# PEER gates through 16-bit one-hots in three parts, a top-16 search over 64 pairs, eleven gathered rows a head, and norms moved in the first and last stage

## What is computed

```python
def block(hc):                                   # 128 tokens at a time
    q = (hc @ wq).reshape(128, 8, 2, 128)
    sc = einsum('thcd,hckd->thck', q, keys)      # 8 heads, 2 halves, 128 keys
    s1, i1 = top_k(sc[:, :, 0], 16)
    s2, i2 = top_k(sc[:, :, 1], 16)
    cand = s1[..., :, None] + s2[..., None, :]   # 256 pairs
    cidx = i1[..., :, None] * 128 + i2[..., None, :]
    top, pos = top_k(cand, 16)
    eidx = take_along_axis(cidx, pos)            # 16 of 16384 experts a head
    gate = softmax(top)
    act = gelu(einsum('thkd,td->thk', u_tab[eidx], hc))
    return einsum('thk,thkd->td', gate * act, v_tab[eidx])
```

## Time and profile before

| | us |
|---|---|
| median of 2 runs | 4164.6 (4156.0 to 4173.3) |
| profiled execution | 4179.5, span 4177.7 |
| PE busy | 3788.4 (91%) |
| DVE busy | 3029.4 (73%) |
| ACT busy, POOL busy | 1375.9, 869.4 |
| granted TensorE clock, mean | 0.949 |

### The profile page before, as it was taken

The page is one execution under the profiler, slowest core; times in us unless marked ns, Lnnn a source line. Parts: engine busy times, 40 slices in busy tenths (PEclk is TensorE's granted clock), DMA queues, the critical chain, the costliest instruction groups (busy, mean ns, idle before and its releaser), DMA issues. The chain is left out here.

```text
span 4177.7 us, 67901 instructions
## 1 busy us (share of the span) xinstructions
PE 3788.4 (91%) x27802; PEld 3460.6 (83%) x27802; DVE 3029.4 (73%) x5310; ACT 1375.9 (33%) x2109; POOL 869.4 (21%) x593
## 2 busy tenths in 40 slices
PE   6878889899998998999999888989999999999997
PEld 4547777699998998999986776669999898899996
DVE  6446455489888987877775646458888897877876
ACT  3442123333333432333334213333333343333332
POOL 3000000011102234444430000001111223544542
PEclk8989989999999999999999989999999999999998
DMA  4741212167776789999961022227777679999994
GB/s 151 262 144 35 99 54 99 61 206 206 208 209 208 270 319 355 338 337 343 349 246 61 22 99 71 91 72 220 211 209 212 213 264 335 359 342 340 338 340 183
DMA packets 319480, 885.61 MB, mean 212 GB/s; under 512 B 29473, under 2 KB 156577, under 8 KB 311745
## 3 DMA queue, kind: packets, MB, share of 16 engines
q1 hardware_dynamic: 245440, 612.80, 43.9%
q0 software_dynamic: 73728, 268.47, 18.0%
HBM read 751.13 MB, written 130.02 MB: 211 GB/s over the span
## 5 line engine op out<-in xcount | busy, mean ns | idle before, releaser
L207 PE MATMUL peer_ps<-peer_h_high,tile_high 128*128 128x384 f32 (+1 forms) x2304 | 797.3, 346 | 35.5 <-DVE peer_h_low L200 16.6
L207 PE MATMUL peer_ps<-gate_high,tile_high 128*128 128x384 f32 x2048 | 709.6, 347 | 96.9 <-DVE tile_low L200 96.8
L2120 POOL DMA_INDIRECT row<-in_peer_u_rows,row_at x256 | 380.9, 1488 | 1969.0 <-DVE row L2352 1202.1
L209 PE MATMUL peer_ps<-peer_h_high,tile_low 128*128 128x384 f32 (+1 forms) x2304 | 788.5, 342 | 0.0
L208 PE MATMUL peer_ps<-peer_h_low,tile_high 128*128 128x384 f32 (+1 forms) x2304 | 788.3, 342 | 0.0
L200 DVE TENSOR_TENSOR tile_low<-tile,tile_high 128x1024 fp32r<-128x1024 f32 x544 | 662.4, 1220 | 157.0 <-ACT tile_high L195 152.2
L208 PE MATMUL peer_ps<-gate_low,tile_high 128*128 128x384 f32 x2048 | 704.0, 344 | 0.0
L209 PE MATMUL peer_ps<-gate_high,tile_low 128*128 128x384 f32 x2048 | 702.9, 343 | 0.0
L195 ACT ACTIVATE tile_high<-tile 128x1024 fp32r<-128x1024 f32 x544 | 571.2, 1050 | 20.1 <-DMA tile<-in_peer_u 19.9
L2120 POOL DMA_INDIRECT row<-in_peer_v,row_at x256 | 454.6, 1776 | 480.0 <-DVE own_sum L2358 437.3
L207 PEld LDWEIGHTS peer_ps<-gate_high,tile_high 128*128 128x128 f32 x2048 | 398.1, 194 | 107.6 <-DVE tile_low L200 107.5
(11 more groups left out here) (453 smaller groups left out, 5476.2 us busy)
## 6 DMA issues: line engine op xcount, KB each, us to landing
tile<-in_peer_u SPq DMA_DIRECT2D x256, 512.0 KB, 4.1
tile<-in_peer_v SPq DMA_DIRECT2D x256, 512.0 KB, 7.1
gates<-gates_out SPq DMA_DIRECT2D x24, 2048.0 KB, 10.1
gates_in<-gates SPq DMA_DIRECT2D x32, 1536.0 KB, 15.9
acts<-up_act SPq DMA_DIRECT2D x240, 192.0 KB, 4.4
act_in<-acts SPq DMA_DIRECT2D x240, 192.0 KB, 8.8
in_w<-in_w_in SPq DMA_DIRECT2D x36, 512.0 KB, 3.6
tile<-in_peer_wq SPq DMA_DIRECT2D x32, 512.0 KB, 4.8
```

The lines of the kernel that those rows point to most:

```text
L207: pe.matmul(out, wh, mh, start=first, stop=False)
L209: return pe.matmul(out, wl, mh, start=False, stop=last)
L2120: pool.indirect_dma_start(row[n % NROW][:, :], None, table, bass.IndirectOffsetOnAxis(ap=row_at[:, n % ROWS:n % ROWS + 1], axis=0)) \
```

## The change

In `peer`: the gate tables are made with 16-bit one-hots. The gate is split into three 16-bit parts that add up to it (`share_gates`, new, four DVE operations a layer), DVE makes one one-hot for each key number and the second times each of the three parts (five operations a group, values laid out keys by tokens, 16 tokens side by side), and PE adds three products a token where there was one. The search for the best 16 of 256 pairs looks at 64 pairs, which hold the best 16 whatever the scores: row 0 with 16, rows 1 to 3 with 8, rows 4 to 7 with 4, rows 8 to 15 with 1. Finding the two key numbers from a position takes other and more small operations. A head takes eleven u rows: six at the sites as before and five in a row at its end (`some_rows(hd, ROWS_BY_HEAD)`), so 77 + 4 + 24 + 16 = 121 come before the down stage and 7 in it; v rows start at tile 10.

In `front`: the products start on activations scaled by the gain alone, and the reciprocal root is multiplied in when DVE, no longer ACT, moves each sum out of PSUM (`take`). The final norm works in two halves of 256 tokens, and its result is stored in eight DMAs.

```diff
+            tile(0)
             for k in range(KD):
                 pe.wait_ge(squared.sem, squared.at(k + 1))
                 last = pe.matmul(ps[7][:, :], pg.c["ones"][:, :], sq[:, k, :], start=(k == 0), stop=(k == KD - 1))
             last.then_inc(summed.sem, 1)
             pe.wait_ge(small_loaded.sem, small_loaded.at(16 * small))
             for j in range(IN_TILES):
-                tile(j)
+                if j:
+                    tile(j)
...
-            def take(j):
-                act.wait_ge(in_summed.sem, in_summed.at(j + 1))
-                i = IN_ORDER[j]
-                if i >= RW_TILES:
-                    act.activation(uT[:, i - RW_TILES, :].rearrange("p (s n) -> p n s", s=SC),
-                                   ps[j % 2][:, :].rearrange("p (n s) -> p n s", s=SC), ACT.Copy).then_inc(in_taken.sem, 1)
-                    return
-                if j >= IN_ZB:
-                    act.wait_ge(shifted.sem, shifted.at(j - IN_ZB + 1))
-                act.activation(zb[j % IN_ZB][:, 1:T + 1], ps[j % 2][:, :], ACT.Copy).then_inc(in_taken.sem, 1)
+            def scaled_high(k):
+                act.activation(rh[:, k, :], pg.xT[:, k, :], ACT.Copy, scale=gain[:, k:k + 1]).then_inc(h_high_made.sem, 1)
...
+            def take(j):
+                i = IN_ORDER[j]
+                dve.wait_ge(in_summed.sem, in_summed.at(j + 1))
+                if i >= RW_TILES:
+                    tokens = lambda x: x.rearrange("p (n s) -> p n s", s=SC)
+                    dve.tensor_tensor(uT[:, i - RW_TILES, :].rearrange("p (s n) -> p n s", s=SC), tokens(ps[j % 2][:, :]), tokens(rstd),
+                                      ALU.mult).then_inc(in_taken.sem, 1)
+                    return
+                if j >= IN_ZB:
+                    dve.wait_ge(shifted.sem, shifted.at(j - IN_ZB + 1))
+                dve.tensor_tensor(zb[j % IN_ZB][:, 1:T + 1], ps[j % 2][:, :], rstd, ALU.mult).then_inc(in_taken.sem, 1)
...
+PLANES = 3
 ROWS = PH * TOPK
 NROW = 6
-ROWS_BY_HEAD, ROWS_BY_GROUP, ROWS_BY_TILE = 6, 1, 1.6
-DOTS_UNTIL = 24
+ROWS_BY_HEAD, ROWS_BY_GROUP, ROWS_BY_TILE = 11, 1, 1.6
+DOTS_UNTIL = 8
+PAIRS = ((0, 1, 16), (1, 3, 8), (4, 4, 4), (8, 8, 1))
+PAIR_AT = [sum(some * wide for _, some, wide in PAIRS[:j]) for j in range(len(PAIRS) + 1)]
+PAIRED = PAIR_AT[-1]
...
-                        last = pe.matmul(ps[2 + n % GBANKS][:, t * NKEY:(t + 1) * NKEY], one[g % 2][:, 4 * c + t, :],
-                                         two[g % 2][:, 4 * c + t, :], start=True, stop=True)
+                        for j in range(PLANES):
+                            last = pe.matmul(ps[2 + n % GBANKS][:, t * NKEY:(t + 1) * NKEY], one[g % 2][:, :, 4 * c + t],
+                                             shares[g % 2][:, j, :, 4 * c + t], start=(j == 0), stop=(j == PLANES - 1))
...
                 dve.tensor_copy(atf[:, :, :, :], at[:, :, :, :])
-                for tb in range(TB):
-                    last = dve.tensor_tensor(cand[:, tb, :, :], down(top[:, tb, 0, :]), across(top[:, tb, 1, :]), ALU.add)
+                at_pair = 0
+                for first, some, broad in PAIRS:
+                    into = cand[:, :, at_pair:at_pair + some * broad].rearrange("p t (a b) -> p t a b", b=broad)
+                    last = dve.tensor_tensor(into, down(top[:, :, 0, first:first + some], broad),
+                                             across(top[:, :, 1, 0:broad], some), ALU.add)
+                    at_pair += some * broad
                 link(last)
                 lows(1)
-                top16([(cand[:, tb, :, :].rearrange("p a b -> p (a b)"), rest[:, tb, :], best[:, tb, own], pos[:, tb, :])
+                top16([(cand[:, tb, :], rest[:, tb, 0:PAIRED], best[:, tb, own], pos[:, tb, :])
                        for tb in range(TB)])
...
-                dve.tensor_scalar(spot[0][:, :, :], pos[:, :, :], 4, None, ALU.logical_shift_right)
-                link(dve.tensor_scalar(spot[1][:, :, :], pos[:, :, :], TOPK - 1, None, ALU.bitwise_and))
-                for j in range(2):
-                    last = dve.tensor_copy(spotf[j][:, :, :], spot[j][:, :, :])
-                link(last)
-                for j in range(2):
-                    for tb in range(TB):
-                        last = dve.tensor_tensor(hit[j][:, tb, :, :], down(spotf[j][:, tb, :]), ramp, ALU.is_equal)
-                link(last)
+                dve.tensor_tensor(steps[:, :, 1:TOPK], atf[:, :, 0, 1:TOPK], atf[:, :, 0, 0:TOPK - 1], ALU.subtract)
+                link(dve.tensor_copy(spotf[0][:, :, :], pos[:, :, :]))
+                dve.tensor_copy(steps[:, :, 0:1], atf[:, :, 0, 0:1])
+                link(dve.tensor_scalar(spotf[1][:, :, :], spotf[0][:, :, :], float(PAIR_AT[1]), None, ALU.is_ge))
+                link(dve.scalar_tensor_tensor(out=spotf[1][:, :, :], in0=spotf[0][:, :, :], scalar=float(PAIR_AT[2]),
+                                              in1=spotf[1][:, :, :], op0=ALU.is_ge, op1=ALU.add))
+                for _ in range(2):
+                    link(dve.scalar_tensor_tensor(out=spotf[1][:, :, :], in0=spotf[0][:, :, :], scalar=float(PAIR_AT[3]),
+                                                  in1=spotf[1][:, :, :], op0=ALU.is_ge, op1=ALU.add))
+                link(dve.tensor_copy(wide[:, :, :], spotf[1][:, :, :]))
+                link(dve.tensor_tensor(spot[:, :, :], mask[:, :, :], wide[:, :, :], ALU.logical_shift_right))
+                link(dve.tensor_tensor(spot[:, :, :], pos[:, :, :], spot[:, :, :], ALU.bitwise_and))
+                dve.tensor_copy(spotf[1][:, :, :], spot[:, :, :])
+                link(dve.tensor_tensor(hit[0][:, :, :, :], down(spotf[0][:, :, :], TOPK), every(starts[:, :]), ALU.is_ge))
                 lows(1)
                 some_rows(hd, 4)
-                for j in range(2):
-                    for tb in range(TB):
-                        last = dve.tensor_tensor(hit[j][:, tb, :, :], hit[j][:, tb, :, :], across(atf[:, tb, j, :]), ALU.mult)
-                link(last)
+                dve.tensor_tensor(hit[1][:, :, :, :], down(spotf[1][:, :, :], TOPK), every(pg.c["ramp"][:, 0:TOPK]), ALU.is_equal)
+                link(dve.tensor_tensor(hit[0][:, :, :, :], hit[0][:, :, :, :], across(steps[:, :, :], TOPK), ALU.mult))
+                link(dve.tensor_tensor(hit[1][:, :, :, :], hit[1][:, :, :, :], across(atf[:, :, 1, :], TOPK), ALU.mult))
                 lows(1)
                 some_rows(hd, 5)
...
+            def share_gates():
+
+                link(dve.tensor_tensor(left[:, :], gate_row[:, :], route[:, 2, :], ALU.subtract))
+                link(dve.tensor_copy(route[:, 3, :], left[:, :]))
+                link(dve.tensor_tensor(left[:, :], left[:, :], route[:, 3, :], ALU.subtract))
+                link(dve.tensor_copy(route[:, 4, :], left[:, :]))
+
             def make_onehots(g):
                 t = slice(g * GROUP, (g + 1) * GROUP)
                 if g >= 2:
                     dve.wait_ge(spread.sem, spread.at((g - 1) * (GROUP // 4)))
-                per_key = lambda j: route[:, j, t].rearrange("p (t k) -> p t k", k=1).to_broadcast([P, GROUP, NKEY])
-                keys_at = pg.c["ramp"][:, :].rearrange("p (t k) -> p t k", t=1).to_broadcast([P, GROUP, NKEY])
-                dve.tensor_tensor(two[g % 2][:, :, :], keys_at, per_key(1), ALU.is_equal)
-                link(dve.tensor_tensor(one[g % 2][:, :, :], keys_at, per_key(0), ALU.is_equal))
-                last = dve.tensor_tensor(two[g % 2][:, :, :], two[g % 2][:, :, :], per_key(2), ALU.mult)
+                per_key = lambda j: route[:, j, t].rearrange("p (k t) -> p k t", k=1).to_broadcast([P, NKEY, GROUP])
+                if g:
+                    dve.wait_ge(onehots_made.sem, onehots_made.at(g))
+                dve.tensor_tensor(two[:, :, :], key_ramp[:, :, :], per_key(1), ALU.is_equal)
+                link(dve.tensor_tensor(one[g % 2][:, :, :], key_ramp[:, :, :], per_key(0), ALU.is_equal))
+                for j in range(PLANES):
+                    last = dve.tensor_tensor(shares[g % 2][:, j, :, :], two[:, :, :], per_key(2 + j), ALU.mult)
                 last.then_inc(onehots_made.sem, 1)
...
             for hd in range(PH):
                 search(hd)
                 lows(BRIDGE + 3 - (PH - 1 - hd) * (UPS_HEAD + 2) - done[0])
+                some_rows(hd, ROWS_BY_HEAD)
...
+            share_gates()
+            link(dve.tensor_copy(key_ramp[:, :, :], pg.c["ramp"][:, :].rearrange("p (k t) -> p k t", t=1)
+                                 .to_broadcast([P, NKEY, GROUP])))
             make_onehots(0)
...
```

More of the change, by code:

```diff
@@ L179, in _, with mean @@
             link = linker(dve, vec_step)
[L180 to L186, removed]
-            link(last)
-    squared.passed(KD)
-    for s in (summed, meaned, rooted):
-        s.passed(1)
+            def mean(h):
+                dve.wait_ge(summed.sem, summed.at(h + 1))
```

(32 more changed lines are left out.)

118 lines of the change are left out of this document (66 added, 52 removed).

## The result

The changed kernel takes **4516.51 us** (median, 4510.91 to 4522.11) against 4164.64 before: the ratio is **1.0845**, 95% interval 1.0732 to 1.0958. The forecast was 4100 with a range up to 4215, so it was wrong in size and in sign. The profiled execution has a span of 4509.2 us, 331.5 more than the 4177.7 before.

The account below looks back on a forecast made before the run. PE was taken as the main bound (91% busy), with DVE close in the one-hot stage and DMA transfers in the down stage. 2 x (-33 - 3 + 8 + 3 - 4) - 7 = -65 us gave 4100 us, range 4050 to 4215.

Parts of the forecast that it names:

- The one-hot stage: One-hot stage of each layer: PE and DVE both near 9.0 us a group after the change, -3 us a layer.
- the price of a gate product: One-hot stage: each one-pass 16-bit product with its own weight load taken at 0.070 us on PE, 48 a group.
- a rival at 0.23 us: One-hot stage: PE's operand reads 32 bytes apart cost about 1.8 ns a value; total +299, 4464 us; chance 0.13.
- Weight loads: One-hot stage: a 16-bit weight load costs PE 0.112 us like a float32 record's; total +27, 4192 us; chance 0.22.
- DVE at one value a cycle: One-hot stage: 16-bit DVE operations get no double pace, 13.8 us a group; total +167, 4332 us; chance 0.04.
- Down stage: Down stage: 35 u row sets a layer move out, easing transfers; 4.35 us for each tile, -33 us a layer.
- Search: Search stage: five rows in a row at a head's end stall PE 1.5 us, seven times; +8 us a layer.
- Bridge: Bridge between search and one-hots: `share_gates` and the wide ramp put DVE work before the first one-hots, +3 us a layer.
- First stage: First stage: PE starts sooner on activations scaled by gain alone, less added waits for `take`; -4 us a layer.
- Last norm: Final norm: two halves hide part of the reciprocal and scaling, and the last DMA is smaller; -7 us once.

Follow-up runs that it names:

- blocks of two tokens: The changed kernel with its 16-bit one-hots held two tokens at a time, one token's values 4 bytes apart for PE instead of 32: 4075.52 us, ratio 0.9804.

## Why the prediction was wrong, by its own steps

**The one-hot stage, forecast -3, measured +208 a layer. The step that failed is the price of a gate product: 0.070 us taken, 0.241 measured.** The sum went from "a pass of 128 columns is 0.056" to the product as if its operands were packed. The distance of the values was put at no cost; it stood in the text only as a rival at 0.23 us (4464 us), with a chance of 0.13, set aside since ACT's and DVE's rows walk 256 bytes a value and TensorE takes a packed float32 value every 0.42 ns. Neither bears on a step of 32 bytes: the cost measured is full from 16 bytes on, and the packed pace says nothing of it. The only strided rows of the trace gave 1.8 ns for both engines, and TensorE's was the same; they should have set the forecast. The rule of the Trainium skill quoted there ("Advanced Engine Details and Errata", SBUF Cachelines) had the right sign: 0.241 us with each value in another line of 16 bytes, 0.056 packed.

The rival itself was 52 us short in all. Its group was 48 x 0.23 + 5.55 = 16.6; with 0.241 it is 17.1 us, 411 a stage. The rest is the clock: behind each group some eight passes start 0.320 and not 0.173 us apart, which with a longer first step is 1.4 us, and 24 times that is 33 us. Together 444, measured 439. No step of mine had a fall of the clock while PE is never idle. What makes the clock fall under these products is not shown.

**Weight loads (0.22)** fell: a load per 16-bit product hides at 0.056 us. What the earlier trace rows shows is a float32 record, 0.112 us for its two passes and loads, half of which is just that 0.056. **DVE at one value a cycle** fell: 1.22 us. The Trainium skill ("VectorE: DVE Perf Modes", the tier table) gives 1224 ns for it, and the trace agrees with 1220.

**The stage before was misread too.** The sum set 9.13 us a group against "the 219 us seen", but 219 is the length of the window in the earlier trace rows, which begins 12 us into the stage. The 32 tiles take 230.6 and 233.3 us, 9.6 to 9.7 a group. With blocks of two tokens, where a product takes 0.058 us (forecast 0.070, bound 0.056), the stage takes 213.8 and 215.3 us, close to the 216 forecast, and DVE's work falls from 9.4 to 8.7 us a group. So at that pace the gain is 17 and 18 us against the kernel before, not 3.

**Down stage, forecast -33, measured -46** (bounds -53 and 0). The mechanism was right, as the run with six rows shows with 46 us by that edit alone. The term was mis-sized: 548.1/128 is 4.28 us a tile and not 4.35. In that the first tile's wait, which I kept at 9.7, is 4.3 in after; with the old one-hots it is 9.1 again and the stage 553.3, so some 5 us of the 46 come with the slow one-hot stage ahead of it.

**Search, forecast +8, measured +21 and +26** (bound +25). "PE stalls 1.5 us, seven times" was too small, and two terms were missing. After's timeline of DVE and PE at a head's end, beside the earlier trace rows:

```profile
1031.68 1.22 DVE L210 TENSOR_TENSOR tile_low<-tile,tile_high 128x1024 fp32r<-128x1024 f32 x1 [4.26 <-ACT tile_high L205]
1032.82 1.22 DVE L2391 SCALAR_TENSOR_TENSOR row<-row,h_own 128x1024 f32<-128x1024 f32 x1
...
1041.66 1.22 DVE L210 TENSOR_TENSOR tile_low<-tile,tile_high 128x1024 fp32r<-128x1024 f32 x1
...
1042.94 0.50 PE L217 MATMUL peer_ps<-peer_h_high,tile_high 128*128 128x512 f32 x1 [2.22 <-DVE tile_low L210]
```

The stall is 2.2 us, and the lead of the tiles behind it, which I called enough, is 1.2 to 2.4 us where six rows leave 4.4 to 5.6, so the whole head runs with less. PE's waits in the search of layer 0, before and then after:

```profile
PE peer_ps L207 <- DVE tile_low L200: 0.5, 1, 0.5
...
PE peer_ps L217 <- DVE tile_low L210: 11.9, 5, 3.5
PE peer_ps L217 <- ACT up_act L2272: 7.2, 9, 1.8
```

So the waits on low parts alone are near the 10 us forecast. What the forecast put at nothing are the longer waits on `up_act` (2.5 before) and the granted clock, 0.98 and 0.97 over the searches of after and 1.00 over those before. By the runs with six and eleven rows the batch cost 19 and not 10; the 64 pairs cost 4 and 8 where I had a gain in DVE's work and none in time.

**Bridge, +3:** +2.9 and +4.3. **First stage, -4:** -5.9 and -5.8; PE's first product now stands 6 us after ACT's first operation, as worked out, and PE waited for `take`'s result (`zb`) once, 0.5 us. Beside the earlier trace rows:

```profile
230.75 2.56 ACT L421 ACTIVATE in_rh<-xT,vec 128x512 fp32r<-128x512 f32 x4 [16.09 <-PEq L1269]
...
236.82 0.80 PE L217 MATMUL front_ps<-in_rh,in_w_high 128*128 128x512 f32 x1 [28.38 <-DVE in_w_low L210]
```

**Last norm, -7:** -6.3; the second half's reciprocal takes 1.67 us in the chain in place of 3.37. The forecast without the one-hots was 2 x (-33 + 8 + 3 - 4) - 7 = -59, and the run with the old ones gave -52 by its ratio. That this agrees is in part luck: the down stage gave more than its term and the search cost more than its own.

## What to carry to other kernels

Price a product by its moving operand's distance in bytes before the number of its columns: in these runs packed 16-bit or float32 values ran at TensorE's full pace, and one value each 16 bytes or more cost 1.7 to 1.8 ns whatever the type. DVE's faster 16-bit pace needed only two neighbours: blocks of two serve both engines, where the transposed layout served DVE alone and was a loss. Put added work where the engine's own trace shows it waiting, and not evenly: against the six rows a head, the same five more cost the search 2 to 4, 16 to 20 or 34 to 39 us a layer by their places.

## What the runs showed of the hardware

- 16-bit moving operand, product of 128 x 128: 0.056, 0.058, 0.116, 0.227, 0.232 us at 2, 4, 8, 16, 32 bytes. Float32: 0.112, 0.114, 0.227, 0.233, 0.218 at 4, 8, 16, 32, 64. One reading fits all ten within 0.012 us: a product takes the longer of its passes and 1.8 ns for each 16-byte stretch that holds a value. The Trainium skill ("SBUF — State Buffer", Specifications (TRN2)) has lines of 16 bytes and wants two hits in each for full bandwidth. The runs agree with 16 bytes, where the cost stops growing (0.227 and 0.232 us at 16 and 32), but not with two hits: 16-bit values 8 bytes apart have two in a line and still run at half pace (0.116 against 0.056).
- The weights' distance costs a 16-bit product at most 0.006 us with a packed moving operand (0.062 against 0.056 us), and 0.009 where the moving operand is at 32 bytes too (0.241 against 0.232). It costs a float32 product as much as the moving operand's: 0.118, 0.233, 0.238, 0.219 us at 8, 16, 32, 64 bytes.
- TensorE's granted clock fell, to a mean of 0.66 to 0.72 over the stretch, under products that started without a gap, when they were 16-bit ones 0.227 us or more apart; it stayed at 1.00 under float32 ones just as far apart, and under 16-bit ones at 0.116.
- DVE keeps 2048 16-bit values in 1.22 us with only two of them neighbours in each run, the other operand repeated over the keys.
